# Attention heads of two layers scored in pairs, and a causal mixer computed without its void quarter

## The reference

```python
s = (jnp.einsum('bhqd,bhkd->bhqk', q_blk, k).astype(jnp.float32) * scale
     + F_blk[..., None] - F[:, :, None, :])
s = jnp.where(kpos[None, :] <= qpos[:, None], s, -jnp.inf)
p = jax.nn.softmax(s, axis=-1).astype(v.dtype)
return jnp.einsum('bhqk,bhkd->bhqd', p, v)
```

## Time and profile before

| | |
|---|---|
| median of three runs | 3412.58 us |
| the profiled execution | 3420.76 us, its span 3419.1 us |
| PE busy | 3290.6 us (96%), 27286 matmul records |
| DVE, ACT busy | 2242.9 us (66%), 1438.2 us (42%) |
| the chain that ended last | PE 87%, DVE 6%, DMA, ACT and issue 2% each |
| mean granted clock of PE | 0.975 of full speed |

### The profile page before, as it was taken

The page is one execution under the profiler, slowest core; times in us unless marked ns, Lnnn a source line. Parts: engine busy times, 40 slices in busy tenths (PEclk is TensorE's granted clock), DMA queues, the critical chain, the costliest instruction groups (busy, mean ns, idle before and its releaser), DMA issues.

```text
span 3419.1 us, 63534 instructions
## 1 busy us (share of the span) xinstructions
PE 3290.6 (96%) x27286; PEld 3188.0 (93%) x27286; DVE 2242.9 (66%) x2339; ACT 1438.2 (42%) x1422; POOL 157.6 (5%) x292
## 2 busy tenths in 40 slices
PE   5999979999999999999999999999999999999998
PEld 5998879999999998878999999999887999999998
DVE  5797877666666586567655555557567765555555
ACT  3253334444444454545443344334444534433433
POOL 2111100000001000011000000000011000000000
PEclk7899999999999999999999999999999999999999
DMA  9788768666666554334555555555344465555553
GB/s 381 281 318 304 270 250 269 219 205 214 207 208 220 185 162 138 124 127 157 195 189 192 196 193 189 195 185 174 123 124 136 162 197 193 189 195 196 189 192 135
DMA packets 320749, 681.68 MB, mean 199 GB/s; under 512 B 14768, under 2 KB 21620, under 8 KB 320164
## 3 DMA queue, kind: packets, MB, share of 16 engines
q1 hardware_dynamic: 286272, 562.74, 49.9%
q0 software_dynamic: 31232, 109.07, 8.8%
q10 hardware_dynamic: 3108, 7.89, 0.6%
HBM read 677.47 MB, written 7.94 MB: 200 GB/s over the span
## 4 chain that ended last, share of the span: by engine, by line
PE 87%; DVE 6%; DMA 2%; ACT 2%; issue 2%; POOL 0%; ACTq 0%; DVEq 0%; POOLq 0%; SPq 0%
PE G L688 52%; PE Dn L688 34%; DVE w_lo L1231 2%; PE Dn L691 1%; DVE ada_acc L1356 1%; DMA zT<-in_w_ada 1%; ACT w_hi L2172 1%; DMA ada_raw<-in_w_ada 1%; DVE sq L1280 1%; DMA raw<-in_w_in 0%; DMA raw<-in_w_out 0%; DVE sq L1947 0%; DVE xT L1961 0%; DMA ada_x<-in_w_ada 0%; PE G L691 0%
## 5 line engine op out<-in xcount | busy, mean ns | idle before, releaser
L688 PE MATMUL G<-h_hi,w_hi 128*128 128x256 f32 x5760 | 1617.4, 281 | 10.0 <-DVE w_lo L1231 5.3
L1231 DVE TENSOR_TENSOR w_lo<-raw,w_hi 128x2048 fp32r<-128x2048 f32 (+2 forms) x536 | 1219.3, 2275 | 609.3 <-ACT w_hi L2172 608.0
L2172 ACT CAST w_hi<-raw 128x2048 fp32r<-128x2048 f32 (+2 forms) x536 | 1017.2, 1900 | 1421.4 <-DMA raw<-in_w_down 424.1
L688 PE MATMUL G<-h_lo,w_hi 128*128 128x256 f32 x5760 | 1603.4, 278 | 0.0
L688 PE MATMUL G<-h_hi,w_lo 128*128 128x256 f32 x5760 | 1603.0, 278 | 0.0
L688 PEld LDWEIGHTS G<-h_hi,w_hi 128*128 128x128 f32 x5760 | 1090.9, 189 | 33.7 <-issue 29.0
L688 PEld LDWEIGHTS G<-h_lo,w_hi 128*128 128x128 f32 x5760 | 1090.9, 189 | 0.4
L688 PEld LDWEIGHTS G<-h_hi,w_lo 128*128 128x128 f32 x5760 | 1090.2, 189 | 0.0
L688 PE MATMUL Dn<-act_hi,w_hi 128*128 128x256 f32 x2752 | 763.2, 277 | 7.3 <-DVE act_lo L1765 7.3
L688 PE MATMUL Dn<-act_lo,w_hi 128*128 128x256 f32 x2752 | 762.8, 277 | 0.0
L688 PE MATMUL Dn<-act_hi,w_lo 128*128 128x256 f32 x2752 | 762.7, 277 | 0.0
(11 more groups left out here) (259 smaller groups left out, 1677.8 us busy)
## 6 DMA issues: line engine op xcount, KB each, us to landing
raw<-in_w_up SPq DMA_DIRECT2D x128, 1024.0 KB, 5.4
raw<-in_w_down SPq DMA_DIRECT2D x128, 1024.0 KB, 5.0
raw<-in_w_in SPq DMA_DIRECT2D x88, 1024.0 KB, 5.3
ada_raw<-in_w_ada POOLq DMA_DIRECT2D x120, 512.0 KB, 6.5
raw<-in_w_ffn_gate SPq DMA_DIRECT2D x44, 1024.0 KB, 5.1
raw<-in_w_ffn_up SPq DMA_DIRECT2D x44, 1024.0 KB, 5.1
raw<-in_w_ffn_down SPq DMA_DIRECT2D x44, 1024.0 KB, 5.0
raw<-in_w_o SPq DMA_DIRECT2D x32, 1024.0 KB, 5.0
```

The source lines that it names most:

```text
L688: return nc.tensor.matmul(o, lhsT, rhs, start=start, stop=stop, skip_group_check=True)
L1231: v.tensor_tensor(w_lo[j][:, 0:m], raw[j][:, 0:PIECE_K * n], w_hi[j][:, 0:m], ALU.subtract).then_inc(lo_done, 1)
L2172: s.copy(w_hi[j][:, 0:PIECE_K * n], raw[j][:, 0:PIECE_K * n]).then_inc(hi_done, 1)
```

## The change

In the layers `head_slots` starts heads in pairs: C12 C13 at 12, then 14, 16, 18, 20, 22, 24; C2 C3 at 25; B at 27, 29, 31, 33; A at 34, 36, 38, 39. Every slot now has three lists: heads to transpose, heads whose output is due, heads to start. The first head of a pair is transposed one piece after its start, the second two pieces after, and the outputs of both stand together in that later slot. Where the next pair starts one piece on ("quick", at 24, 33, 38 and 39), both are transposed and finished in the next slot. A pair is scored by turns (first head's upper half, second head's upper half, then the lower halves), where at most one head is transposed in the slot; at 25, 34 and 39 it is scored head by head between the transposes as before.

In the first mixer the first half of queries is scored against 128 keys only, the mask is added, exponentials and scalings are done on these alone, the void transposed block is dropped (three transposes, 384 columns copied), and the output product for keys 128 to 255 has 128 columns. DVE fills the void quarter of both `s_sb` buffers once with -1e30, at hook 28.

```diff
-    starts = {12: "C12", 13: "C13", 14: "C14", 15: "C15", 16: "C8", 17: "C9", 18: "C10", 19: "C11",
-              20: "C4", 21: "C5", 22: "C6", 23: "C7", 24: "C0", 25: "C1", 26: "C2 C3",
...
+    starts = {12: "C12 C13", 14: "C14 C15", 16: "C8 C9", 18: "C10 C11", 20: "C4 C5", 22: "C6 C7", 24: "C0 C1",
...
+    slots, seq = {p: ([], [], []) for p in range(12, 41)}, 0
+    for p, names in starts.items():
+        pair = []
+        for name in names.split():
+            pair.append((seq, name[0], int(name[1:])))
...
+        slots[p][2].extend(pair)
+        quick = p + 1 in starts or p + 1 == 40
+        slots[p + 1][0].extend(pair if quick else pair[:1])
+        if not quick:
+            slots[p + 2][0].extend(pair[1:])
+        slots[p + 1 if quick else p + 2][1].extend(pair)
...
+CAUSAL_BLOCKS = [(0, 0), (0, 1), (1, 1)]
...
+        PT_F = PT.rearrange("p a b -> p (a b)")[:, 0:3 * P]
+        pT_F = [x[:, :, :].rearrange("p a b -> p (a b)")[:, 0:3 * P] for x in pT]
...
+                    if kind == "F":
+                        for n, (k, t) in enumerate(CAUSAL_BLOCKS):
+                            i = turn(PT_F[:, n * P:(n + 1) * P], s_sb[H % 2][:, t, k * P:(k + 1) * P])
+                        i.then_inc(pt_done, 1)
+                        return
...
-                    o, v = MISC, v_tok[:, :, h * P:(h + 1) * P]
+                    mm(MISC, v_tok[:, 0, h * P:(h + 1) * P], pT_F[H % 2][:, 0:2 * P], True, False)
+                    return mm(MISC[:, P:2 * P], v_tok[:, 1, h * P:(h + 1) * P], pT_F[H % 2][:, 2 * P:3 * P], False, True)
...
+            def score(H, kind, h, t):
+                if kind == "F":
+                    n = P * (t + 1)
+                    mm(SC[H % 2][:, t, 0:n], zT[:, Z_Q + h, t * P:(t + 1) * P], zT[:, Z_K + h, 0:n], t == 0, False)
+                    return mm(SC[H % 2][:, t, 0:n], neg1[:, :], f_m[h % 2][:, 0:n], False, True)
...
+                return mm(SC[H % 2][:, t, :], zT[r0:r0 + 64, qt_, t * P:(t + 1) * P], zT[r0:r0 + 64, kt_, :],
+                          t == 0, t == 1)
...
+            def score_pair(new, base):
+                for H, kind, h in new:
+                    score_waits(kind, h, base + H)
+                for t in range(QT):
+                    for H, kind, h in new:
+                        i = score(H, kind, h, t)
+                        if t == QT - 1:
+                            i.then_inc(qk_done, 1)
+
+            def slot(trans, outs, new, base):
+
+                pair = len(new) == 2 and len(trans) < 2
+                for n in range(max(len(trans), len(new))):
+                    if n < len(trans):
+                        H, kind, h = trans[n]
                         finish(H, kind, h, base + H, 0)
-                    if n < len(new):
+                    if n < len(new) and not pair:
                         H, kind, h = new[n]
                         scores(H, kind, h, base + H)
-                if done:
-                    misc_open(out_name(done), mbase[0])
-                    for H, kind, h in done:
+                if pair:
+                    score_pair(new, base)
+                if outs:
+                    misc_open(out_name(outs), mbase[0])
+                    for H, kind, h in outs:
                         i = finish(H, kind, h, base + H, 1)
                     i.then_inc(misc_w, 1)
...
-                    i = v.tensor_scalar(s_sb[b][:, t, :], s_sb[b][:, t, :], rinv[:, b, t:t + 1], None, ALU.mult)
+                    w = P * (t + 1) if kind == "F" else T
+                    i = v.tensor_scalar(s_sb[b][:, t, 0:w], s_sb[b][:, t, 0:w], rinv[:, b, t:t + 1], None, ALU.mult)
...
                     for t in range(QT):
-                        i = v.scalar_tensor_tensor(out=s_sb[b][:, t, :], in0=SC[b][:, t, :], scalar=f_t[:, t, h:h + 1],
-                                                   in1=causal[:, t, :], op0=ALU.add, op1=ALU.add)
+                        w = P * (t + 1)
+                        i = v.scalar_tensor_tensor(out=s_sb[b][:, t, 0:w], in0=SC[b][:, t, 0:w],
+                                                   scalar=f_t[:, t, h:h + 1], in1=causal[:, t, 0:w],
+                                                   op0=ALU.add, op1=ALU.add)
...
+            def blank_future():
+                dve.wait_ge(misc_w, misc_no["pool3"] + 1)
+                for b in range(2):
+                    v.memset(s_sb[b][:, 0, P:], -1e30)
+            hook(28, blank_future)
...
-                    s.copy(pT[H % 2][:, :, :], PT).then_inc(pt_copied, 1)
+                    if kind == "F":
+                        s.copy(pT_F[H % 2], PT_F).then_inc(pt_copied, 1)
+                    else:
+                        s.copy(pT[H % 2][:, :, :], PT).then_inc(pt_copied, 1)
...
+                    if kind == "F":
+                        for t in range(QT):
+                            w = P * (t + 1)
+                            i = s.activation(s_sb[b][:, t, 0:w], s_sb[b][:, t, 0:w], ACT.Exp, bias=negmax[:, b, t:t + 1],
+                                             scale=1.0, accum_out=rsum[:, b, t:t + 1])
+                        i.then_inc(exp_done, 1)
+                        continue
```

More of the change, by code:

```diff
@@ L133, in head_slots @@
 def head_slots():
-    starts = {12: "C12", 13: "C13", 14: "C14", 15: "C15", 16: "C8", 17: "C9", 18: "C10", 19: "C11",
[3 rows of a table removed]
[L139 to L143, removed]
-            seq += 1
[L145 to L148, removed]
+    starts = {12: "C12 C13", 14: "C14 C15", 16: "C8 C9", 18: "C10 C11", 20: "C4 C5", 22: "C6 C7", 24: "C0 C1",
+              25: "C2 C3", 27: "B4 B5", 29: "B6 B7", 31: "B0 B1", 33: "B2 B3", 34: "A0 A1", 36: "A2 A3",
+              38: "A4 A5", 39: "A6 A7"}
+    slots, seq = {p: ([], [], []) for p in range(12, 41)}, 0
[3 more added lines that the diff above has]
+            pair.append((seq, name[0], int(name[1:])))
+            seq += 1
+        slots[p][2].extend(pair)
[4 more added lines that the diff above has]
+        slots[p + 1 if quick else p + 2][1].extend(pair)
+    assert seq == 32
     return slots
 SLOTS2 = head_slots()
+CAUSAL_BLOCKS = [(0, 0), (0, 1), (1, 1)]
 SLOTS1 = {}
@@ L157 @@
     _new = [(START1[_p], "F", START1[_p])] if _p in START1 else []
[L158 removed]
+    SLOTS1[_p] = (_done, _done, _new)
 def out_name(done):
     return f"out_{done[0][1]}{done[0][0]}"
[L166 removed]
+OUT_OF = {(kind, H): out_name(done) for slots in (SLOTS1, SLOTS2) for _, done, _ in slots.values()
           for H, kind, h in done}
[L168 to L170 removed]
+OUT1 = sum(1 for _, done, _ in SLOTS1.values() if done)
+OUT2 = sum(1 for _, done, _ in SLOTS2.values() if done)
+KIND2 = {H: kind for _, done, _ in SLOTS2.values() for H, kind, h in done}
 ORDER1 = [(0, 0), (0, 1), (1, 0), (1, 1), (0, 2), (0, 3), (1, 2), (1, 3)] + [(g, j) for g in range(2, 9) for j in range(4)]
@@ L859, in finish, with score_waits @@
                 return i
-            def scores(H, kind, h, no):
+            def score_waits(kind, h, no):
                 if kind == "F":
-                    if H >= 2:
+                    if no >= 2:
                         pe.wait_ge(exp_done, no - 1)
@@ L866, in scores @@
                     pe.wait_ge(fm_ready, h + 1)
[L867 to L870, removed]
                     return
@@ L882, in scores @@
+            def scores(H, kind, h, no):
+                score_waits(kind, h, no)
                 for t in range(QT):
-                    i = mm(SC[H % 2][:, t, :], zT[r0:r0 + 64, qt_, t * P:(t + 1) * P], zT[r0:r0 + 64, kt_, :],
-                           t == 0, t == 1)
+                    i = score(H, kind, h, t)
                 i.then_inc(qk_done, 1)
[L887 to L891, removed]
+            def score_pair(new, base):
[3 more added lines that the diff above has]
+                    for H, kind, h in new:
+                        i = score(H, kind, h, t)
+                        if t == QT - 1:
+                            i.then_inc(qk_done, 1)
@@ L899, in slot @@
                         i = finish(H, kind, h, base + H, 1)
                     i.then_inc(misc_w, 1)
-            for p, (done, new) in SLOTS1.items():
-                hook(p, slot, done, new, 0)
+            for p, (trans, outs, new) in SLOTS1.items():
+                hook(p, slot, trans, outs, new, 0)
             for half in range(4, 10):
@@ L1111, in _ @@
                         hook(p, v_turn, z, evac)
-                    for p, (done, new) in SLOTS2.items():
-                        hook(p, slot, done, new, l * HEADS2 + HEADS1)
+                    for p, (trans, outs, new) in SLOTS2.items():
+                        hook(p, slot, trans, outs, new, l * HEADS2 + HEADS1)
                     for kind in "CBA":
@@ L1678, in _ @@
             last1 = MIX1_PIECES
-            for p, (done, new) in SLOTS1.items():
+            for p, (done, _, new) in SLOTS1.items():
                 hook(p, slot, done, [], 0)
@@ L2029, in _ @@
                         hook(Q_ALT_AT + 1, q_end, z)
```

(10 more changed lines are left out.)

12 lines of the change are left out of this document (6 added, 6 removed), and 2 rows, old and new, of the table starts.

## The result

The changed kernel takes 3367.05 us (median of 5 runs, 3361.89 to 3373.76), beside 3412.99 us for the kernel before; the ratio is 0.9863, 95% interval 0.9849 to 0.9878. That is some 46 us less, where 29 had been forecast. It lies 1 us inside the lower end of the range of 3366 to 3403, and outside the forecast's own 3376 to 3394. The profiled executions, 3420.76 and 3373.76 us, differ by 47.0.

What follows compares the result with a forecast made beforehand. PE, busy 96% of the span, was taken to bound the kernel. Pairs (-24.6 us, both layers) and the first mixer (-4.5) sum to -29.1, against the median of 3412.58 a forecast of 3384, range 3366 to 3403.

Steps and rivals of the forecast that it cites:

- Pairs share their time on PE: Layers' mixers: a second head's scores or outputs cost PE nothing right behind its neighbour's; two heads' scores take 1.07 us.
- Rival 2: Paired scores: turns do not run side by side, each pair takes 2.12 us; 3411, no change; chance 0.08.
- C part, -12.5 a layer: Slots 12 to 26: score units 15 to 9, output units 14 to 7, transposes 14 to 15; -12.5 us per layer.
- The wait of 0.4 us: Slots 15 and 23: two row maxima ahead of a square-root chain make DVE later than PE; 0.4 us booked.
- B and A, +0.2 a layer: Slots 27 to 39: +3.4 and -3.9 us, +0.2 together; PE's savings from pairs eaten by DVE and the clock.
- chain of waits: B heads: DVE's long row maxima make PE wait about 4.6, 3 and 2.2 us at slots 28, 30 and 32.
- the half clock: Slots 28, 30, 32, 34: after each wait PE runs some 6.8 us at 1.2 GHz, costing up to 3.4 us.
- Rival 1: Slots 30 and 32: new waits do not bring the clock down; -2.0 and -3.3 us, twice, 3373; chance 0.2.
- rival 3: B part: half clock lasts on from wait to wait, three more pieces lose up to 2.7 us; 3400; chance 0.15.
- rival 4: C heads: DVE and ACT late for every first head, 16 slots with waits above 2 us; 3470; chance 0.04.
- First mixer, -4.5: First mixer's eight heads: halved products and one transpose fewer save PE 5.7 us; 4.5 booked, bounds 0 and 7.
- The 0.2 taken from the transpose: First mixer: a product cut from 256 to 128 columns saves 0.2 us, judged by a 128-column transpose of 0.11 per record.

Runs made afterwards that it cites:

- e3: Changed kernel with a pair's four score products issued head after head instead of by turns; 3369.68 us, 0.9877 of the kernel before.
- e1: Kernel before with only the first mixer's part of the change, layers' heads one by one; run twice, ratios 0.9993 and 0.9983.

## Why the prediction was right, and where its size was off

*Pairs share their time on PE.* Right: 1.07 and 1.02 us a pair. Rival 2 fell by the rows above and by e3.

*C part, -12.5 a layer.* Measured -14.0 in layer 1, and -15.6 in layer 2, where the kernel before also lost 1.7 us at half clock. The wait of 0.4 us that I booked at slots 15 and 23 did not come: PE waits for no `s_sb` there. The other 1.1 us is a term mis-sized. A slot without scores and outputs is 2.26 us shorter than one with them (slot 15: 6.33 in place of 8.59), not 2.07, because transposes take 0.36 us ahead of a piece and 0.53 ahead of scores; 6 x 0.19 = 1.1.

*B and A, +0.2 a layer.* This is the step that failed: measured -9.8 and -3.6. Its chain of waits held, its clock did not. From slot to slot in layer 1:

| slots | forecast | measured |
|---|---|---|
| 27 to 28 | 12.9 | 13.01 |
| 28 to 29 | 10.2 | 8.80 |
| 29 to 30 | 12.5 | 12.49 |
| 30 to 31 | 10.1 | 8.11 |
| 31 to 32 | 10.6 | 10.65 |
| 32 to 33 | 9.7 | 6.19 |
| 33 to 34 | 10.4 | 10.48 |
| 34 to 35 | 14.1 | 11.00 |
| 35 to 39 | 34.5 | 34.27 |

Each row that ends in a wait or hangs on DVE is right to 0.2 us. The four rows behind a wait, for which I booked the half clock, are wrong by 1.4, 2.0, 3.5 and 3.1 us: 10.0 together, which is the whole miss of layer 1.

In slots 28 and 30 the clock did fall, but not all of it cost PE time. In slot 28 two of the 6.8 us at half clock fell within the wait itself. In slot 30 it lasted 3.4 us and not the 6.8 that I took, and cost nothing: in layer 2 of e3 the clock did not fall there, PE came 1.34 us early to slot 31, and 30 to 31 took 8.08 us all the same. DVE's chain sets that length. In slots 32 and 34 the clock did not fall in this layer. Layer 2 is the same up to slot 34, where it fell: 14.77 us from 34 to 35.

Rival 1 (8.1 and 6.4 us for 30 to 31 and 32 to 33) described these slots better than the forecast did, though for slot 30 not by its reason, since the clock mostly fell there. Its time, 3373, is also the nearer one. Its chance of 0.2 was too low: the argument for the fall was one wait of 2.09 us in one layer. Layer 2 of the same trace had the same fall, and the waits of 2.30 us at slot 28 brought one in both layers too, four of four; yet over eight layers the wait of 2.09 us did it in five. That the range still held the result, by 1 us, is in part luck: the most that any rival gave B and A beyond the forecast was rival 1's 10.6 us for both layers, and it came to 13.8, with 4.6 more in the C part that nothing had booked. Of rival 3, a half clock that lasts on, there is only slot 34 of layer 2; rival 4 fell with the C part, where no wait came.

*First mixer, -4.5.* The product of 128 columns costs 0.32 us, so 0.21 less, and 8 x (3 x 0.21 + 0.11) = 5.9; measured -5.5 in the trace and -5.8 and -2.4 over runs. The 0.2 taken from the transpose was a good neighbour. The estimate from the Trainium skill's page ("TensorE: Matmul & The Clock Gate", "LDWEIGHTS (loading the stationary operand)"), 5.9, agrees with the trace: 0.21 us less for each halved product. Where the other 0.4 us went was not traced.

*The sum.* Between the profiled runs, -47.0 stands against -29.1. Of the difference of 17.9, 13.8 is B and A, 4.6 the C part and 1.0 the first mixer. The other 1.5 or so is given back elsewhere: 3.2 us ahead of layer 1, where the half clock took 18.8 us in place of 15.4, less what the other stretches gained.

## What to carry to other kernels

Put products that use different halves of TensorE's rows or columns right behind one another, whatever their order, and put the outputs where something covers the copy that they wait for. Where two heads share a chain, do the work of the one that is needed later behind the work of the one that is waited for: that gave a further 7 to 9 us here, none of it in the A heads, and 14 with the evacuations moved into DVE's wait as well. Book a clock that falls behind a wait by how often it does so in several layers and runs, not by one example.

## What the runs showed of the hardware

Four f32 transposes of 128 x 128 take 0.36 us when a piece follows them, 0.43 when an f32 product on all 128 rows does, and 0.53 when one on 64 rows does. Two f32 products on different halves of the rows start 0.01 us apart, whether they are issued by turns or head after head. A stretch at 1.2 GHz in the layers' mixers lasted 3.4 to 10.2 us, which is 1.7 to 5.1 us less of PE's clock; part of it can fall in time in which PE waits anyway. The same wait of 2.09 us brought the clock down in five layers and left it alone in three. With heads one by one, slots 27 to 39 of both layers took 247.8 us in the kernel before and 241.8 in the second run of e1, with the same program there; half clock took 15.4 us of the one and 6.8 of the other. The weights behind the first mixer make another 9 us (882.1 and 891.0 us for one kernel), so one pair of profiled runs tells less than the medians do.
